# Last mixer's values, queries and keys: from twelve weight units of 256 columns to six pairs of units of 512 columns, one token tile and eight heads per item, in four banks

## What is computed

```python
def mixer_c(h, w_in, forget_bias, q_norm_g, k_norm_g, w_out):
    proj = h @ w_in                       # (256, 1024) @ (1024, 4112)
    q, k, v, gate, f_logit = split_cols(proj, [1024, 1024, 1024, 1024, 16])
    q = rms_norm_2(q.reshape(b, t, 16, 64), q_norm_g) * (64 ** -0.5)
    k = rms_norm_2(k.reshape(b, t, 16, 64), k_norm_g)
    v = v.reshape(b, t, 16, 64)
    log_f = jax.nn.log_sigmoid((f_logit + forget_bias).astype(f32))
    cum = jnp.transpose(jnp.cumsum(log_f, axis=1), (0, 2, 1))
    ...
        s = s + cum[:, :, q0:k_end, None] - cum[:, :, None, :k_end]
        prob = jax.nn.softmax(jnp.where(mask, s, -jnp.inf), axis=-1)
    ...
    o = o * jax.nn.sigmoid(gate)
    return o @ w_out
```

## Time and profile before

| | us |
|---|---|
| median of 3 runs | 1869.79 (1867.84 to 1870.37) |
| span of the profiled execution | 1870.4 |
| time of the execution at the top of the three | 1870.37 |
| PE busy | 1825.3 (98%) |
| DVE busy | 1176.3 (63%) |
| ACT busy | 887.6 (47%) |

### The profile page before, as it was taken

The page is one execution under the profiler, slowest core; times in us unless marked ns, Lnnn a source line. Parts: engine busy times, 40 slices in busy tenths (PEclk is TensorE's granted clock), DMA queues, the critical chain, the costliest instruction groups (busy, mean ns, idle before and its releaser), DMA issues.

```text
span 1870.4 us, 25829 instructions
## 1 busy us (share of the span) xinstructions
PE 1825.3 (98%) x10816; PEld 1565.8 (84%) x10816; DVE 1176.3 (63%) x1458; ACT 887.6 (47%) x1091; POOL 50.4 (3%) x107
## 2 busy tenths in 40 slices
PE   7999999999999998999999999999999999999998
PEld 7998898888888887888788898888788889788887
DVE  5346775588888897655468955555654456745454
ACT  4434451377767775544322345444444345535442
POOL 0040000000000000000000000000000010000000
PEclk9989999899999999999999999999999999999999
DMA  8343334589999896654333017555555434236540
GB/s 356 136 158 113 113 137 152 198 335 348 347 354 342 320 354 258 230 193 174 122 135 113 25 36 279 198 184 182 201 182 189 170 136 158 91 111 241 190 175 37
DMA packets 51523, 363.58 MB, mean 194 GB/s; under 512 B 5712, under 2 KB 5840, under 8 KB 8784
## 3 DMA queue, kind: packets, MB, share of 16 engines
q1 hardware_dynamic: 51264, 359.83, 52.0%
q10 hardware_dynamic: 144, 2.10, 0.3%
HBM read 360.86 MB, written 1.05 MB: 193 GB/s over the span
## 4 chain that ended last, share of the span: by engine, by line
PE 89%; DVE 6%; ACT 3%; issue 1%; POOL 0%; DMA 0%; DVEq 0%; SPq 0%; POOLq 0%; ACTq 0%
PE bank L2635 8%; PE bank L2637 8%; PE bank L2636 8%; PE bank L2173 8%; PE bank L2660 4%; PE bank L2662 4%; PE bank L2661 4%; PE bank L2227 4%; PE bank L2527 3%; PE bank L2529 3%; PE bank L2528 3%; PE bank L2212 3%; PE bank L2358 3%; PE bank L2450 3%; PE bank L2542 2%; PE bank L2544 2%
## 5 line engine op out<-in xcount | busy, mean ns | idle before, releaser
L1305 DVE TENSOR_TENSOR w_a<-ring,w_a 128x2048 fp32r<-128x2048 f32 x221 | 504.2, 2290 | 276.9 <-ACT w_a L814 276.4
L814 ACT ACTIVATE w_a<-ring 128x2048 fp32r<-128x2048 f32 x221 | 420.2, 1912 | 187.8 <-PE bank L2662 90.1
L2635 PE MATMUL bank<-w_a,h 128*128 128x512 f32 x536 | 212.7, 397 | 6.0 <-DVE h L1369 6.0
L2637 PE MATMUL bank<-w_a,h 128*128 128x512 f32 x536 | 209.2, 390 | 0.0
L2636 PE MATMUL bank<-w_a,h 128*128 128x512 f32 x536 | 208.8, 390 | 0.0
L1305 DVE TENSOR_TENSOR w_b<-ring,w_b 128x2048 fp32r<-128x2048 f32 x62 | 142.1, 2291 | 67.8 <-ACT w_b L814 67.2
L2173 PE MATMUL bank<-h,w_a 128*128 128x256 f32 x1088 | 147.2, 291 | 1.7 <-DVE ring_lo L1404 1.0
L2173 PEld LDWEIGHTS bank<-h,w_a 128*128 128x128 f32 x1088 | 138.7, 197 | 4.9 <-issue 3.8
L814 ACT ACTIVATE w_b<-ring 128x2048 fp32r<-128x2048 f32 x62 | 118.6, 1913 | 45.7 <-PE bank L2662 25.7
L1077 ACT ACTIVATE sil<-bank,tiny 128x256 f32<-128x256 f32 x88 | 41.7, 474 | 175.2 <-PE bank L2637 175.2
L2635 PEld LDWEIGHTS bank<-w_a,h 128*128 128x128 f32 x536 | 100.7, 188 | 27.1 <-DVE h L1369 4.9
(11 more groups left out here) (473 smaller groups left out, 3270.0 us busy)
## 6 DMA issues: line engine op xcount, KB each, us to landing
ring<-in_stream SPq DMA_DIRECT2D x330, 1024.0 KB, 4.8
G<-in_gains SPq DMA_DIRECT2D x15, 512.0 KB, 5.6
cmp_area<-in_cmp_w ACTq DMA_DIRECT2D x1, 2048.0 KB, 10.8
sm<-in_small SPq DMA_DIRECT2D x1, 1582.0 KB, 13.0
con<-in_consts SPq DMA_DIRECT2D x1, 1032.0 KB, 16.8
X<-in_x SPq DMA_DIRECT2D x2, 512.0 KB, 4.9
out_x<-X SPq DMA_DIRECT2D x4, 256.0 KB, 2.0
sm<-in_small SPq DMA_DIRECT2D x1, 730.5 KB, 23.0
```

The costliest lines, as they stand in the source:

```text
L814: act.activation(w_slot(unit)[:, 0, :], ring[:, unit % RING, :], ACT.Copy).then_inc(S("w_hi"), 1)
L1305: dve.tensor_tensor(w_slot(unit)[:, 1, :], ring[:, unit % RING, :], w_slot(unit)[:, 0, :].bitcast(FP32), ALU.subtract).then_inc(S("w_lo"), 1)
L2635: pe.matmul(bank[4 + t][:, :], x_hi, w[0][:, k, :], start=first, stop=False)
L2637: ins = pe.matmul(bank[4 + t][:, :], x_lo, w[0][:, k, :], start=False, stop=end)
```

## The change

The twelve units of values, queries and keys become six pairs. A pair (i = 0 to 5) has 512 columns, eight heads; its first unit holds rows 0 to 511 of the weights, its second rows 512 to 1023. An item j = 2i + t is one pair for one token tile: `c_part(i, t, half)` is 12 matmuls of 512 columns (4 blocks of rows x 3 products), and two parts (half 0 and 1) make an item. Items go to banks 0, 1, 6, 5 in turn (banks 0 and 1 are also those of the scores). Items 0 to 3 are values; items 4 to 11 take the places n = 0 to 7 of the chain, with the same instruction counts and sizes on ACT and DVE. The first item of a pair is complete after `c_part(i, 0, 1)` (new use of `part_full`), the second after `c_part(i, 1, 1)`. Units, bytes and the order of the splits stay. A turn now covers four head pairs of one token tile, so the scores of the first four head pairs need turns 0, 1, 4 and 5, and the others need all.

```diff
+    units += wide_units(c_in[:, 2048:3072]) + wide_units(c_in[:, 0:2048]) + list(column_units(c_in[:, 3072:4096]))
+        def c_bank(j):
+            return (0, 1, 6, 5)[j % 4]
@@ ACT
+            def item_ready(j):
+                if j % 2 == 0:
+                    act.wait_ge(S("part_full"), len(PARTS) + j // 2 + 1)
+                else:
+                    act.wait_ge(S("unit_used"), D_UNITS["c"] + j + 1)
@@ PE
-            for n in range(2):
-                split_tokens(group_begin(f"c{8 + n}"), "c", n, range(0, 1))
+            def c_part(i, t, half):
+                unit, item = D_UNITS["c"] + 2 * i + half, 2 * i + t
+                w = parts(unit, 4)
+                lo_ready(unit)
+                if half == 0 and item >= 4:
+                    pe.wait_ge(S("proj_free"), GI["c8"] + item - 3)
+                for k in range(4):
+                    x_hi, x_lo = (x[:, 4 * half + k, t * P:(t + 1) * P] for x in (h_hi, h_lo))
+                    ps = bank[c_bank(item)][:, :]
+                    pe.matmul(ps, x_hi, w[0][:, k, :], start=(half == 0 and k == 0), stop=False)
+                    pe.matmul(ps, x_hi, w[1][:, k, :], start=False, stop=False)
+                    ins = pe.matmul(ps, x_lo, w[0][:, k, :], start=False, stop=(half == 1 and k == 3))
+                if t == 1:
+                    ins.then_inc(S("unit_used"), 1)
+                elif half == 1:
+                    ins.then_inc(S("part_full"), 1)
...
-            for n in range(2, 4):
-                split_tokens(group_begin(f"c{8 + n}"), "c", n)
+            for half in range(2):
+                for t in range(TT):
+                    c_part(1, t, half)
...
-            for n in range(8):
-                split_tokens(group_begin(f"c{n}"), "c", 4 + n)
-                if n:
-                    turn_heads(n - 1)
+            for i in range(2, 6):
+                c_part(i, 0, 0)
+                c_part(i, 1, 0)
+                if i > 2:
+                    turn_heads(2 * i - 6)
+                c_part(i, 0, 1)
+                if i > 2:
+                    turn_heads(2 * i - 5)
+                c_part(i, 1, 1)
+            turn_heads(6)
...
-                pe.wait_ge(S("side_free"), SI[f"hs{4 + p // 2}"] + 1)
+                pe.wait_ge(S("side_free"), SI[f"hs{5 + 2 * (p // 4)}"] + 1)
```

More of the change, by code:

```diff
@@ L148, in row_units, with wide_units @@
     return w.reshape(-1, 2, P, D).transpose(0, 2, 1, 3).reshape(-1, P, UNIT)
+def wide_units(w):
+    return list(w.reshape(2, 4, P, -1, 2 * UC).transpose(3, 0, 2, 1, 4).reshape(-1, P, UNIT))
 def gated_units(gate, up, down):
@@ L218, in lay_out @@
     units += gated_units(fg[1, 0], fu[1, 0], fd[1, 0])
-    c_in = column_units(a["c_w_in_2"][0][:, :4096])
-    units += [c_in[n] for n in C_ORDER]
+    c_in = a["c_w_in_2"][0]
+    units += wide_units(c_in[:, 2048:3072]) + wide_units(c_in[:, 0:2048]) + list(column_units(c_in[:, 3072:4096]))
     units += list(column_units(a["c_w_out_2"][0]))
@@ L1223, in _ @@
             f_rows = slice(0, F_COPIES * N_FOX)
+            def item_ready(j):
[3 more added lines that the diff above has]
+                    act.wait_ge(S("unit_used"), D_UNITS["c"] + j + 1)
             for n in range(4):
                 split_ahead("c", n, C_SPLIT)
-                evac(f"c{8 + n}", f_v[:, :, n * UC:(n + 1) * UC], ACT.Copy, scale=0.5)
+                item_ready(n)
+                act.activation(f_v[:, n % 2, n // 2 * 512:n // 2 * 512 + 512], bank[c_bank(n)][:, :], ACT.Copy, scale=0.5)\
+                   .then_inc(S("proj_free"), 1)
                 if n == 2:
@@ L1236, in turned_out @@
                 act.wait_ge(S("side_full"), SI[f"hs{n}"] + 1)
-                act.activation(fq[:, 2 * n:2 * n + 2, :], tiles(bank[7][:, :], 2), ACT.Copy,
+                act.activation(fq[:, 4 * (n // 2):4 * (n // 2) + 4, n % 2 * P:(n % 2 + 1) * P], tiles(bank[7][:, :], 4), ACT.Copy,
                                scale=(qg8 if n < 4 else P2("kg"))[:, 0:1]).then_inc(S("side_free"), 1)
@@ L1241, in _ @@
                 split_ahead("c", 4 + n, C_SPLIT)
-                act.wait_ge(S(FULL[f"c{n}"][0]), FULL[f"c{n}"][1])
+                item_ready(4 + n)
                 if n >= 2:
                     act.wait_ge(S("qk_ss"), n - 1)
-                act.activation(f_sq[:, n % 2, :], bank[5 + GI[f"c{n}"] % 2][:, :], ACT.Square).then_inc(S("f_sq"), 1)
+                act.activation(f_sq[:, n % 2, :], bank[c_bank(4 + n)][:, :], ACT.Square).then_inc(S("f_sq"), 1)
                 if n:
@@ L2060, in scaled_out @@
                 heads = lambda x: x.rearrange("p (h d) -> p h d", d=HD)
-                dve.tensor_tensor(heads(q_tok[:, n % 2, :]), heads(bank[5 + GI[f"c{n}"] % 2][:, :]),
+                dve.tensor_tensor(heads(q_tok[:, n % 2, :]), heads(bank[c_bank(4 + n)][:, :]),
                                   rs.unsqueeze(2).to_broadcast([P, 8, HD]), ALU.mult).then_inc(S("proj_free"), 1)
@@ L2975, in _ @@
             pe.wait_ge(S("h_lo"), HI0["c"] + 2)
-            for n in range(2):
-                split_tokens(group_begin(f"c{8 + n}"), "c", n, range(0, 1))
+            def c_part(i, t, half):
[15 more added lines that the diff above has]
+            for half in range(2):
+                c_part(0, 0, half)
             keep_busy(8)
@@ L2981, in _ @@
             pe.wait_ge(S("h_lo"), HI0["c"] + 4)
-            for n in range(2):
-                split_tokens(bank[5 + GI[f"c{8 + n}"] % 2], "c", n, range(1, 2))
+            for half in range(2):
+                c_part(0, 1, half)
             pe.wait_ge(S("h_32"), H32["c"] + 4)
@@ L2994, in turn_heads @@
                 pe.wait_ge(S("proj_free"), GI[f"c{n}"] + 1)
[L2995 to L2998, removed]
+                for c in range(4):
+                    ins = pe.transpose(ps[:, c * P:(c + 1) * P], q_tok[:, n % 2, c * P:(c + 1) * P], C("ident"))
                 ins.then_inc(S("side_full"), 1)
-            for n in range(8):
-                split_tokens(group_begin(f"c{n}"), "c", 4 + n)
-                if n:
-                    turn_heads(n - 1)
+            for i in range(2, 6):
[8 more added lines that the diff above has]
+            turn_heads(6)
             def gate_quarter(j):
@@ L3018, in _ @@
             pe.wait_ge(S("f_cum"), 1)
-            pe.wait_ge(S("proj_free"), GI["c11"] + 1)
+            pe.wait_ge(S("proj_free"), GI["c5"] + 1)
             def fox_scores(p):
-                pe.wait_ge(S("side_free"), SI[f"hs{4 + p // 2}"] + 1)
+                pe.wait_ge(S("side_free"), SI[f"hs{5 + 2 * (p // 4)}"] + 1)
                 if p:
```

## The result

| | before | after |
|---|---|---|
| median | 1870.83 us (8 runs, 1867.21 to 1874.63) | 1879.31 us (8 runs, 1875.88 to 1882.35) |
| ratio after / before | | 1.0041, interval 1.0029 to 1.0054 |
| second comparison, on another occasion | 1872.60 us (17 runs) | 1879.56 us (12 runs), ratio 1.0030, 1.0015 to 1.0044 |
| span of the profiled execution | 1870.4 | 1880.6 |

The change makes the kernel slower by 0.3 to 0.4%, 5.6 to 7.7 us, and both intervals exclude no change. The forecast had said slower by 4.0, 1873.8, with a range up to 1876.8. A run's time and the span of its core are not the same number: over all runs on record the time is 1.7 to 1.9 us above the span (1882.35 for the profiled 1880.6). The profiled execution of the kernel before, with its span of 1870.4, is therefore one of about 1872.2 us, and not the highest of the first three runs.

What follows compares the result with a forecast made beforehand. The prediction took PE's own list and its waits for DVE to bound the last mixer. Full-clock terms summed to +2.2 us, plus 1.8 for the clock gave +4.0: 1873.8 us against the median 1869.79, range 1871.3 to 1876.8.

Steps and rivals of the forecast that it cites:

- part 5: Wait of 4.6 us ahead of unit 8 makes PE's clock fall to half rate; loses 1.8 us, ends 0 and 3.4.
- the step from the stage to the median: Later start of the attention loop is passed on whole; forecast 1873.8 against the median 1869.79.
- All four waits: PE waits ahead of units 6, 8, 10 and turn 6: 1.05, 4.6, 0.55 and 1.5 us.
- Part 1: Wide for narrow matmuls in the last mixer: -4.0 us, and +0.6 for parts after four transposes.
- Parts 2 to 4: Late DVE chains make PE wait 1.05 (unit 6), 4.6 (unit 8), 0.55 (unit 10) and 1.5 us (turn 6).
- The two old waits: PE's waits ahead of turns 2 and 7 for DVE's scaling, 1.6 and 0.5 us start to start, go.
- The sum at full clock: Matmul saving, parts after transposes, four new waits, less two old ones: +2.2 us, allowed +1.0 to +3.4.
- The upper end: Clock loss behind unit 8's wait if the whole 6.9 us low stretch lies in work: 3.4 us.
- the forecast's own case: Clock falls once behind unit 8's wait, costing 0.7 to 2.6 us; 1872.4 to 1875.5, chance 0.55.
- The clock holds: Rival: all four waits come but the clock holds or dips momentarily; +2.2 to +2.9 us, chance 0.13.
- The clock falls twice: Rival: clock falls again at turn 6's wait; +5.6 to +7 us, chance 0.19 including staying low.
- The wide matmuls win: Rival: DVE reaches squares_in 2 before PE finishes unit 7; -2.4 us, 1867.4, or 1864.3; chance 0.08.

Runs made afterwards that it cites:

- e2: Changed kernel with 19 calls of a 128x128 identity matmul on PE in the wait ahead of unit 8; 1876.52 us against 1873.64 before, ratio 1.0015.
- e6: Kernel before the change with forget_3 on DVE ahead of the loop over the eight items; single execution 1873.52 us, stage 148.1.
- e4: Changed kernel, DVE reordered: low parts ahead of squares_in, forget_3 cut in two, last three low parts in the attention loop; 1869.72 us against 1873.64 before, ratio 0.9980.
- e8: Kernel before the change (narrow units) with DVE's list in the order of e4; ratio 0.9998, stage 147.6 us.
- e3: Changed kernel with each wide matmul done as two of 256 columns; single execution 1880.00 us, stage 157.5.
- e5: Changed kernel with DVE's low part of a unit ahead of squares_in, forget_3 still behind item n = 1; single execution 1873.26 us, stage 152.3.

## Why the prediction was wrong

- **Direction and mechanism were right.** What failed are one term's size, the clock (part 5), and the step from the stage to the median, which was put at nothing. The saving of the wide matmuls is smaller than what late work of DVE costs. All four waits came in the order named.
- **Part 1, the rates.** Forecast -4.0 and +0.6. The three restarts behind waits cost 0.14 us each (1563.73 - 1558.15 = 5.58 for two parts of 2.72), as parts after a turn do. I had counted the turns only; that is +0.4. The rates themselves held.
- **Parts 2 to 4, the waits.** Forecast 1.05, 4.6, 0.55, 1.5. Measured from possible to real start: 1.0, 4.6, 0.55 and 1.5. The chain of 11.06 us from turn 0 to unit 8 measured 11.00. The two old waits went, as forecast.
- **The sum at full clock.** Forecast +2.2, measured +2.8 with the clock held (e2). Of the 0.6 between them 0.4 are the restarts behind waits. The other 0.2 is covered by two restarts more, behind the second input transposes (24 wide matmuls from 1526.29 to 1531.87, 5.58 instead of 5.44 us) and behind `f` (96 from 1535.13 to 1557.11, 21.98 instead of 21.76); the narrow matmuls lost 0.04 in the first of these places.
- **Part 5, the clock: the term that was too small.** Forecast 1.8, taken between 1.6 and 2.1 from one stretch at 1504. Measured 2.8, 2.7 and 2.8 in the repeats (8.2 and 8.4 us for the parts up to turn 2 against 5.6). The step was to let the clock fall 2.0 us into the wait because it had done so at 1504, and to stay low for the 6.9 us seen there. It stayed low for 6.8, but fell 3.7 us into the wait, so nearly all of it fell on work. The moment is not fixed even at the place it was taken from: in the twelve profiles the fall there came 2.0 to 4.1 us after PE went idle, in ten of them only when that wait of 2.4 us was over. Nor is the length: the trace before has low stretches of 3.4 us too, 366.0 to 369.4 and 932.6 to 936.0. One row was read as a rule. The upper end that I had named, 3.4, was the right one to forecast near; the forecast's own case ended at 2.6.
- **From the stage to the median: the step that was put at nothing.** The stage's loss of 5.6 on 1869.79 gives 1875.4, inside the range. The median came out at 1879.3, 5.5 above the forecast: 0.6 is the sum at full clock, 1.0 the clock behind unit 8, 1.0 the reference (1870.83 for eight runs instead of 1869.79 for three), and the other 2.9 (2.1 by the ratio) is not of the stage, which repeats to 0.2 us. The prediction took the rest of the program as fixed; at one and the same program the spans outside the stage differ by 9 us (1730.4 in the second profile of the changed kernel, 1721.1 in the third). The first comparison gave 7.7 by its ratio, the second 5.6; the intervals overlap and both hold 5.6. That the 2.1 us between them are moments at which the clock happened to be low elsewhere fits the 4.6 us outside the stage in the first pair of profiles, but for the medians it is argued, not shown. The range should have had room for it: the kernel before alone has medians of 1869.79, 1870.83, 1871.68, 1872.60 and 1873.64 us on the occasions of this record.
- **The rivals.** "The clock holds" is what e2 made by force: +2.8. "The clock falls twice" did not come: turn 6's 1.33 us left it high. "The wide matmuls win" needs more than `forget_3` out of the way: with that alone the stage is 0.7 under before, but 1.0 over the narrow kernel with the same edit (e6). With the low parts ahead of the squares as well (e4) the wide items are 1.5 ahead of the narrow ones in the same order (e8), and 3.7 ahead of before.

## What to carry to other kernels

An edit that changes the grain of one engine's work moves the deadlines of all the work queued for it. For each low-rate piece in another engine's list, write down from which event it can start and which instruction waits behind it; here 5.7 us of harmless work became the bound because its start was tied to a turn that now stood behind two parts of the next unit, 24 wide matmuls: turn 0 came 40.1 us after the start of the stage instead of 35.0. Before a change to PE's grain, move such pieces to where their engine idles, and price a long wait of PE (here 3.9 us and more) at up to half of the longest half-rate stretch that the trace shows, on top of itself.

## What the runs showed of the hardware

- Waits of 3.9 to 4.4 us with PE idle brought its clock from 2.4 to 1.2 GHz every time (five profiles: the changed kernel's three, e3 and e5). It fell 3.1 to 3.7 us into the wait. The low stretch lasted 3.4 us in one profile and 6.8 in the other four; the work in it was 3.2 to 6.1 us, at a cost of 1.5 to 2.8. Waits of up to 1.5 us in this stage never did it.
- Ahead of the stage, where PE waits 2.4 us, does eight transposes and waits 1.4 to 1.6 us again, the clock fell in all twelve profiles, 2.0 to 4.1 us after PE first went idle, and stayed low for 6.8 to 6.9 us.
- 38 records of dummy matmuls of 128 columns in a wait held the clock at 1.00 and did not delay the real work.
- The first wide matmuls behind four transposes or behind a wait cost a further 0.13 to 0.14 us here: 12 took 2.85 instead of 2.72, 24 took 5.58 instead of 5.44.
- The same program's profiled spans differed by 9 us (1876.6, 1880.6, 1885.7), while the stage differed by 0.2. For an effect of this size the stage in one profile told more than the medians of 8 to 12 runs.
